# Hybrid gMLP and MoBA step: RMSNorm of the MoE router applied in the copies of rows, first expert pair's rows by one-hot products

## The reference

```python
def hier_moe(x, norm_g, w_rg, b_rg, w_re, b_re, w_gate, w_up, w_down):
    h = rms_norm(x, norm_g)
    lg = h @ w_rg + b_rg                       # 4 expert groups, top 1
    le = h @ w_re + b_re                       # 16 experts, top 2 inside the group
    ...
    for e in range(16):
        he = silu(h @ w_gate[e]) * (h @ w_up[e])          # 1024 -> 512
        y = y + gates[..., e:e + 1] * (he @ w_down[e])    # 512 -> 1024
```

## Time and profile before

| | |
|---|---|
| median of 3 runs | 1044.44 us (1040.47 to 1045.44) |
| profiled execution, own time | 1046.14 us |
| its span, first to last instruction | 1044.4 us |
| mean granted TensorE clock | 0.941 |
| TensorE matmul busy | 935.9 us, 90% |
| VectorE busy | 397.7 us, 38% |
| ScalarE busy | 158.9 us, 15% |
| GpSimd busy | 68.1 us, 7% |
| DMA | 327.42 MB, 313 GB/s mean |
| chain that ended last | PE 74%, VectorE 11%, DMA 6%, issue 5% |

### The profile page before, as it was taken

The page is one execution under the profiler, slowest core; times in us unless marked ns, Lnnn a source line. Parts: engine busy times, 40 slices in busy tenths (PEclk is TensorE's granted clock), DMA queues, the critical chain, the costliest instruction groups (busy, mean ns, idle before and its releaser), DMA issues.

```text
span 1044.4 us, 12577 instructions
## 1 busy us (share of the span) xinstructions
PE 935.9 (90%) x4275; PEld 530.1 (51%) x4275; DVE 397.7 (38%) x1828; ACT 158.9 (15%) x400; POOL 68.1 (7%) x93
## 2 busy tenths in 40 slices
PE   6999999977999988998999999766996999988897
PEld 5888888755444443344443334334765344444334
DVE  2235440051133322024697856887024133322014
ACT  2112010030100000002323220223221000000001
POOL 3000200021000000000000000000012000000000
PEclk9999999996999999999998999766996999999999
DMA  9903636063999999999669989998633899999991
GB/s 362 383 28 127 212 132 284 0 249 136 366 379 424 423 421 419 420 417 391 271 234 339 401 332 409 411 409 348 259 134 111 324 386 427 420 420 419 419 418 72
DMA packets 62431, 327.42 MB, mean 313 GB/s; under 512 B 6184, under 2 KB 6408, under 8 KB 51992
## 3 DMA queue, kind: packets, MB, share of 16 engines
q1 hardware_dynamic: 56752, 312.56, 74.5%
q0 software_dynamic: 4720, 11.77, 3.5%
q10 hardware_dynamic: 896, 2.30, 0.6%
HBM read 324.14 MB, written 6.52 MB: 317 GB/s over the span
## 4 chain that ended last, share of the span: by engine, by line
PE 74%; DVE 11%; DMA 6%; issue 5%; ACT 1%; SPq 1%; POOL 1%; ACTq 0%; DVEq 0%; POOLq 0%
PE bank L1197 20%; PE bank L979 11%; PE bank L1223 9%; PE bank L1279 6%; PE bank L1033 6%; DMA ring<-in_moe_w_gate 5%; DVE ring L1729 4%; PE bank L1178 4%; PE bank L1430 3%; PE bank L1394 2%; DVE xT L1672 2%; PE bank L1296 1%; PE bank L1104 1%; PE bank L974 1%; PE bank L1255 1%
## 5 line engine op out<-in xcount | busy, mean ns | idle before, releaser
L1197 PE MATMUL bank<-ring,arena 128*64 128x512 f32 x1024 | 234.7, 614 | 25.7 <-issue 24.3
L1197 PEld LDWEIGHTS bank<-ring,arena 128*64 128x64 f32 x1024 | 84.8, 141 | 172.8 <-issue 170.8
L979 PE MATMUL bank<-arena,ring 128*128 128x264 f32 x512 | 118.8, 389 | 0.1
L1223 PE MATMUL bank<-ring,arena 128*64 128x512 f32 x512 | 113.4, 595 | 2.0 <-ACT arena L740 2.0
L1729 DVE CUSTOM_DVE_ANT_0 ring<-ring,bank 128x128 f32<-128x128 f32 x512 | 110.8, 280 | 9.1 <-PE bank L1296 7.7
L1679 DVE TENSOR_TENSOR arena<-arena,bank 128x512 f32<-128x512 f32 x16 | 11.0, 688 | 248.7 <-PE bank L1197 248.7
L979 PEld LDWEIGHTS bank<-arena,ring 128*128 128x128 f32 x512 | 95.6, 190 | 15.9
L1279 PE MATMUL bank<-ring,arena 128*128 128x512 f32 x192 | 93.4, 637 | 1.2 <-ACT arena L848 1.2
L1223 PEld LDWEIGHTS bank<-ring,arena 128*64 128x64 f32 x512 | 36.2, 137 | 67.9 <-issue 65.5
L1178 PE MATMUL bank<-arena 128*128 128x264 f32 x256 | 63.4, 393 | 1.8 <-ACT arena L745 1.7
L1279 PEld LDWEIGHTS bank<-ring,arena 128*128 128x128 f32 x192 | 37.1, 202 | 52.1 <-issue 49.2
(11 more groups left out here) (245 smaller groups left out, 844.9 us busy)
## 6 DMA issues: line engine op xcount, KB each, us to landing
ring<-in_moe_w_gate SPq DMA_DIRECT2D x32, 2048.0 KB, 22.1
ring<-in_moe_w_up SPq DMA_DIRECT2D x32, 2048.0 KB, 17.8
ring<-in_moe_w_down SPq DMA_DIRECT2D x32, 2048.0 KB, 15.0
ring<-in_cache_k SPq DMA_DIRECT2D x64, 512.0 KB, 7.8
ring<-in_cache_v SPq DMA_DIRECT2D x64, 512.0 KB, 6.5
ring<-in_a_w_in SPq DMA_DIRECT2D x7, 2048.0 KB, 34.5
ring<-in_a_w_out SPq DMA_DIRECT2D x4, 2048.0 KB, 8.4
ring<-in_w_kv SPq DMA_DIRECT2D x4, 2048.0 KB, 16.0
```

Source lines behind the costliest of these rows:

```text
L979: return mm(bank[:, 0:T], slot(base + k // 2, 2)[:, k % 2, j * P:(j + 1) * P], hT[:, k, :], start=(k == 0), stop=(k == KT - 1))
L1197: last = mm(bank[64 * e:64 * e + 64, :], hg[:, int(odd), k, CAP * e:CAP * (e + 1)], slot(base + e, KT)[:, k, :], start=(k == 0), stop=(k = ...
L1223: last = mm(PB[4 + half][64 * e:64 * e + 64, :], heT[:, f, CAP * e:CAP * (e + 1)], slot(down[0] + e, FT)[:, f, 512 * half:512 * (half + 1) ...
```

## The change

- The reciprocal over 128x264 ahead of each router is gone, and the logits are copied unscaled. TensorE turns row 0 of the roots into a column per tile of tokens (three products with a 1), VectorE takes the reciprocals there (rs_t, one number for each token) and applies them in the step that adds the bias.
- GpSimd's eight scalings are gone. TensorE turns the unscaled stream, and ScalarE's copies into hr carry rs_t as the scale.
- The first pair's rows are not gathered from HBM. TensorE multiplies the one-hot of pair 0 with hr, three tiles of tokens for each half of the width, 512 columns at a time; ScalarE and VectorE copy the halves into gr, and the transposes of that pair follow from there. The second and later pairs are gathered as before. gr has moved to other columns of the arena.
- `keep_clock` is called with 4 in both places instead of 10 and 12, the first after the logits' transposes.
- The iota starts at 1, so that the rank needs no subtraction. The copies of gates for the first two pairs stand ahead of the rank, and the maximum behind the one-hots.

```diff
@@ constants
-    put("iota", np.tile(np.arange(CAP), (P, 1)))
+    put("iota", np.tile(np.arange(CAP) + 1.0, (P, 1)))
@@ GpSimd, moe
-                for k in range(KT):
-                    nc.gpsimd.tensor_tensor(hT[:, k, :], hT[:, k, :], rstd, ALU.mult).then_inc(h_made, 1)
...
                 pool.wait_ge(h_stored, 48 * (l + 1))
-                gather(0, 0)
-                gather(1, 1)
                 pool.wait_ge(many_set, l + 1)
...
-                    for i in range(2, NPAIR):
+                    for i in range(1, NPAIR):
                         gather(i, i % 2)
@@ ScalarE, moe
+                act.wait_ge(rstd_made, 2 * l + 1)
...
-                                         PB[4 + i % 4][0:n, :].rearrange("q (p k) -> q k p", k=KT), ACT.Copy)\
+                                         PB[4 + i % 4][0:n, :].rearrange("q (p k) -> q k p", k=KT), ACT.Copy,
+                                         scale=rs_t[0:n, t:t + 1])\
...
+                act.wait_ge(turned[l], 1)
+                nc.scalar.activation(gr[:, 0, 0:D // 2], PB[0][:, :], ACT.Copy).then_inc(hg_lo[l], 1)
@@ TensorE, moe
-                keep_clock(10)
                 pe.wait_ge(lgT_made, l + 1)
...
-                    last = tr(PB[2][0:n, t * 20:(t + 1) * 20], lgT[0:NGRP + NE, t0:t0 + n], ident[0:20, 0:20])
+                    tr(PB[3][0:n, t * 20:(t + 1) * 20], lgT[0:NGRP + NE, t0:t0 + n], ident[0:20, 0:20])
+                keep_clock(4, PB[0])
+                pe.wait_ge(rms_made, 2 * l + 1)
+                for t, (t0, n) in enumerate(TILES):
+                    last = mm(PB[3][0:n, 60 + t:61 + t], rms[0:1, t0:t0 + n], ones[0:1, 0:1], start=True, stop=True)
                 last.then_inc(lg_out, 1)
...
-                    pe.wait_ge(gr_load[l][b], 16 * (n + 1))
+                    if b == 0 and isinstance(n, int) and n == 0:
+                        pe.wait_ge(hg_lo[l], 1)
+                        pe.wait_ge(hg_hi[l], 1)
+                    else:
+                        pe.wait_ge(gr_load[l][b], 16 * (n + b))
...
                 pe.wait_ge(hr_kept, 6 * l + 6)
+                pe.wait_ge(hot_made[l], 1)
+                for half in range(2):
+                    for t, (_, n) in enumerate(TILES):
+                        last = mm(PB[half][:, :], hot[0:n, 0, t, :], hr[0:n, t, 512 * half:512 * (half + 1)],
+                                  start=(t == 0), stop=(t == 2))
+                    last.then_inc(turned[l], 1)
                 owners(0, 0)
                 owners(1, 1)
-                keep_clock(12)
+                keep_clock(4, PB[6])
@@ VectorE, moe
-                v.tensor_tensor(lgT[0:NGRP + NE, :], PB[3][0:NGRP + NE, 0:T], rstd[0:NGRP + NE, :], ALU.mult)\
-                    .then_inc(lgT_made, 1)
+                v.tensor_copy(lgT[0:NGRP + NE, :], PB[3][0:NGRP + NE, 0:T]).then_inc(lgT_made, 1)
...
+                ran(v.reciprocal(rs_t[:, 0:2], PB[3][:, 60:62]))
+                v.reciprocal(rs_t[0:NS, 2:3], PB[3][0:NS, 62:63]).then_inc(rstd_made, 1)
...
+                for t, (_, n) in enumerate(TILES):
+                    ran(v.scalar_tensor_tensor(out=lg[0:n, t, :], in0=PB[3][0:n, t * 20:(t + 1) * 20],
+                                               scalar=rs_t[0:n, t:t + 1], in1=bias[0:n], op0=ALU.mult, op1=ALU.add))
...
-                link(v.tensor_scalar(rank, rank, -1.0, None, ALU.add))
...
                 onehot(0, 0)
                 onehot(1, 1)
+                v.tensor_reduce(many[:, :], counted[:, 2, :], AX.X, ALU.max).then_inc(many_set, 1)
+                dve.wait_ge(turned[l], 2)
+                v.tensor_copy(gr[:, 0, D // 2:D], PB[1][:, :]).then_inc(hg_hi[l], 1)
                 owner_rows(0, 0, 0)
@@ VectorE, before and after each moe
-            normed(0, [])
...
-            normed(2, [])
```

More of the change, by code:

```diff
@@ L228, in small @@
             return region(ro - n, *shape)
-        gm, pg, mn, m1, m2, e2, w1, w2 = (small(3) for _ in range(8))
+        gm, pg, mn, m1, m2, e2, w1, w2, rs_t = (small(3) for _ in range(9))
         ohg, oh1, oh2, leg, le2, cand, ex = (small(3, 4) for _ in range(7))
@@ L1039, in _, with keep_clock @@
             sum_and_route(0, sqB, KT - 1)
-            def keep_clock(n):
+            def keep_clock(n, bank):
                 for _ in range(n):
-                    mm(PB[0][:, 0:P], ident, ident, start=True, stop=True)
+                    mm(bank[:, 0:P], ident, ident, start=True, stop=True)
             def turn_y(k):
@@ L1113, in moe @@
                 with pe.If(flag > LIMIT):
-                    pe.wait_ge(gr_load[l][0], 64)
+                    pe.wait_ge(gr_load[l][0], 48)
                     for k in range(KT):
                         if k >= 2:
-                            pe.wait_ge(hg_hi[l], k - 1)
+                            pe.wait_ge(hg_hi[l], k)
+                        elif k == 0:
+                            pe.wait_ge(hg_lo[l], 1)
+                            pe.wait_ge(hg_hi[l], 1)
                         for t, (t0, n) in enumerate(TILES):
@@ L1242, in moe @@
                 pe.nop()
-            moe(0, 0)
+            moe(0)
             def sample_part(m, h, h_base, banks):
@@ L1436, in _ @@
             sum_and_route(1, sqM, KT - 1)
-            moe(1, 3 * KT)
+            moe(1)
         @block.vector
@@ L1545, in moe @@
                 dve.wait_ge(lgT_out, l + 1)
-                v.tensor_tensor(lgT[0:NGRP + NE, :], PB[3][0:NGRP + NE, 0:T], rstd[0:NGRP + NE, :], ALU.mult)\
-                    .then_inc(lgT_made, 1)
-                link(v.tensor_copy(marks[:, :, :, 2], bc(const("token").unsqueeze(1), [P, 2, 3])))
+                v.tensor_copy(lgT[0:NGRP + NE, :], PB[3][0:NGRP + NE, 0:T]).then_inc(lgT_made, 1)
+                ran(v.tensor_copy(marks[:, :, :, 2], bc(const("token").unsqueeze(1), [P, 2, 3])))
+                ran(v.memset(rs_t, 0.0))
                 link(v.memset(lg, 0.0))
@@ L1551, in moe @@
                 bias = rbias[:, l, :]
-                ran(v.tensor_tensor(lg[:, 0:2, :], PB[2][:, 0:40].rearrange("p (t n) -> p t n", t=2),
-                                    bc(bias.unsqueeze(1), [P, 2, NGRP + NE]), ALU.add))
-                link(v.tensor_tensor(lg[0:NS, 2, :], PB[2][0:NS, 40:60], bias[0:NS], ALU.add))
+                ran(v.reciprocal(rs_t[:, 0:2], PB[3][:, 60:62]))
+                v.reciprocal(rs_t[0:NS, 2:3], PB[3][0:NS, 62:63]).then_inc(rstd_made, 1)
+                settle()
+                dve.wait_ge(rstd_made, 2 * l + 1)
+                for t, (_, n) in enumerate(TILES):
+                    ran(v.scalar_tensor_tensor(out=lg[0:n, t, :], in0=PB[3][0:n, t * 20:(t + 1) * 20],
+                                               scalar=rs_t[0:n, t:t + 1], in1=bias[0:n], op0=ALU.mult, op1=ALU.add))
+                settle()
                 lgg = lg[:, :, 0:NGRP]
@@ L1602, in moe @@
                                      bc(oh1.unsqueeze(2), g44), ALU.mult))
+                for b in range(2):
+                    v.tensor_copy(marks[:, b, :, 0:2], gates[:, :, 2 * b:2 * b + 2])
                 dve.wait_ge(rank_out, l + 1)
                 counted = PB[3][:, 0:3 * NE].rearrange("p (t e) -> p t e", t=3)
-                v.tensor_reduce(many[:, :], counted[:, 2, :], AX.X, ALU.max).then_inc(many_set, 1)
                 link(v.scalar_tensor_tensor(out=rank, in0=counted, scalar=1.0, in1=chose, op0=ALU.add, op1=ALU.mult))
-                link(v.tensor_scalar(rank, rank, -1.0, None, ALU.add))
                 def onehot(i, b):
@@ L1612, in onehot @@
                         dve.wait_ge(owner_out[l], i - 1)
-                    v.tensor_copy(marks[:, b, :, 0:2], gates[:, :, bass.ds(2 * i, 2)])
+                        v.tensor_copy(marks[:, b, :, 0:2], gates[:, :, bass.ds(2 * i, 2)])
                     v.tensor_tensor(hot[:, b, :, :].rearrange("p t (e s) -> p t e s", e=2),
@@ L1621, in owner_rows @@
                     dve.wait_ge(owner_out[l], i + 1)
-                    if not (isinstance(i, int) and i < 2):
-                        dve.wait_ge(gr_load[l][b], 16 * n)
+                    if not (isinstance(n, int) and n - 1 + b < 1):
+                        dve.wait_ge(gr_load[l][b], 16 * (n - 1 + b))
                     v.tensor_scalar(row_of[b][:, 0:1], PB[7][:, 2:3], 1.0 * EMPTY, None, ALU.add)
```

37 lines of the change are left out of this document (17 added, 20 removed).

## The result

| | before | after |
|---|---|---|
| median, side by side | 1045.06 us (7 runs, 1040.47 to 1051.35) | 1054.76 us (7 runs, 1049.37 to 1058.03) |
| profiled execution, own time | 1046.14 us | 1058.03 us |
| its span | 1044.4 us | 1056.2 us |
| mean granted clock | 0.941 | 0.932 |

A forecast was written before the change was run, and what follows sets the result against it. Product and load chains both start at each layer's first gate product, which the router bounds. Layer 0's -3.3 and layer 1's +0.9 gave -2.4 us, from the 1044.44 us median to 1042.0 us; range 1034 to 1047.

The forecast's parts named there:

- Lock of VectorE lifted, "-4.9": In each router, a VectorE step of 5.10 us no longer waits out GpSimd's eight scalings: 4.9 us less.
- ScalarE's "+0.3": Before the first one-hot, ScalarE's six row copies with a scale per partition add 0.3 us (bounds 0 and 0.5).
- Products, "7.6 us": Twelve one-hot passes per layer start at 1.2 GHz, reach full clock after 4.6 us: 7.6 us (all half clock 10.6).
- Dense products brought the clock back within 6 us both times: Argument against the low-clock rival: the clock rose 5.7 and 3.5 us after the gate products began.
- Owners, "1.1": After the one-hot products: pair 0's owner products at full clock 0.8 us, VectorE's two copies 0.3, together 1.1 us.
- Sending, flag and branch, "0.3 + 0.7 + 3.9": After the owners: sending 14 passes 0.3 us, flag load and register steps 0.7, branch over the all-tokens code 3.9.
- no bound of its own: Rival: the branch only waits for the queue to drain; -6.2 us, 1035.8 us, chance 0.12.
- From the branch to the gate product, "2.8": After the branch: transposes, their two copies and the first gate product at half clock, 2.8 us in each layer.
- The sum: Change in time to the first gate product: layer 0 -3.3 us, layer 1 +0.9 us, total -2.4 us.
- The claim that the router reaches the end one for one: Any shift of the first gate product in either layer shifts the kernel's end by the same amount.
- the clock stays low through the products and into the first pair: Rival: half clock in products, owners and first gate products costs 5.6 us per layer; 1053.2 us, chance 0.05.

The follow-up runs named there:

- fill_ahead: Changed kernel plus two groups of filler products (24 and 20 passes) where TensorE waits ahead of the one-hot products; 1041.89 us, ratio to before 1.0001.
- full_tile: Changed kernel with the third tile of tokens in the one-hot products read over all 128 partitions instead of 8; 1047.27 us, ratio to before 1.0042.
- full_early: all_three without the fillers ahead of ranks and products; 1036.05 us, ratio to before 0.9925.
- full_late: Changed kernel with the edits of full_tile and late_code together; 1041.36 us, ratio to before 0.9979.
- shift_code: Changed kernel with 24 nops at the start of TensorE's program; 1056.0 us, ratio to before 1.0132.
- late_code: Changed kernel with 12 filler products at the start of TensorE's program, to move its later code; 1046.22 us, ratio to before 1.0014.
- branch_early: Changed kernel with the second pair's owner products moved behind the branch, into both sides, and four fillers dropped; 1042.78 us, ratio to before 0.9999.
- all_three: Changed kernel with the edits of full_tile, fill_ahead and branch_early together; 1031.81 us, ratio to before 0.9882.
- norm_only: Kernel before with only the norm's part of the change, first pair still gathered, fillers of 10 and 12 kept; 1042.19 us, ratio to before 0.9976.
- norm_lean: norm_only without the ten fillers ahead of the transposes of logits; 1039.46 us, ratio to before 0.998.

## Why the prediction was wrong

- **Lock of VectorE lifted, "-4.9": right.** The step took 0.17 us, the first one-hot came 4.25 us earlier in layer 0 (forecast 4.4). Layer 1 gave 3.48: ScalarE's "+0.3" was 0.9 too small there, as its store's issue took 1.47 us instead of 0.53. The bound of 0.5 looked at the scale of the copies only, not at the stores between them.
- **Products, "7.6 us": the step that failed.** 11.47 and 11.46. "Dense products brought the clock back within 6 us both times" was read from gate products, and taken as a property of the clock. All twelve passes at half clock are 10.6 us by the forecast's own upper bound, 3.0 more than it counted. The other 0.9 the bound left out: passes of different shape follow each other less closely (5.97 against 5.39 us at full clock), and the earlier trace rows, with 9.0 us for 16 passes, gave 0.56 us each for 8 rows, not the 0.44 that was read as the same. Together 3.9 us more in each layer. That the clock sets the size is shown by fill_ahead. Without fillers, it rose midway in all six stretches of full_tile, full_early and full_late; with the 8-row tile, of eight (changed kernel, shift_code, late_code, branch_early) it stayed low in three, rose late in one and midway in four. The idle time just before the products does not explain this: where it was 2.9 us or less, the clock rose midway in five of five stretches without the 8-row tile and in one of five with it. That the 8-row tile is what makes it uncertain rests on these few counts and on three pairs of kernels that differ in it (1.0042 and 1.0088, 0.9925 and 0.9999, 0.9979 and 1.0014, the 8-row tile slower each time); it is likely, not shown. Whether by the gaps between its passes or by the few rows at work is open. The Trainium skill, TensorE: Matmul & The Clock Gate, Part 1, says that sustained matmul activity releases the throttle; three stretches here, of 11.5 us of products each, did not follow it.
- **Owners, "1.1": 1.8** in both layers, because they ran at the low clock (1.44 instead of 0.83).
- **Sending, flag and branch, "0.3 + 0.7 + 3.9": right.** From the second owners to the branch 0.9 and 0.8 us, the branch 3.83 and 3.76. branch_early shows that the branch is a delay of its own, which is what the rival "no bound of its own" denied.
- **From the branch to the gate product, "2.8": right in layer 0 (2.9), 6.9 in layer 1, the second step that failed.** The pause of 4.1 us was in no term and no rival. It goes when the code alone is moved (late_code). From that, and from its distance to the second transfer of code, which is that of the branch to the first, I read it as a second fetch, of the next piece of code, which the first transposes ran into; no run shows the fetch itself to be the cause. The Trainium skill, Runtime: NRT & Kernel Launch, Instruction fetch mechanics, describes refills in blocks of 16 KiB, purely sequential prefetch, and a stall at a taken branch that leaves the fetched window. The branch's 3.8 us and the transfer inside it (0.02 MB) agree; that execution can stall again behind the target is a reading of these traces.
- **The sum.** Layer 0: -3.3 + 3.9 + 0.7 = +1.3. Layer 1: +0.9 + 3.9 + 0.7 + 4.1 + 0.9 for the one-hot, less 0.5 in the hand-offs, the sending and the branch = +10.0. The claim that the router reaches the end one for one held on the whole: 11.3 of 11.8 us here, 14.0 against 13.4 in all_three; over all profiles the two differ by up to 3.6 us (shift_code: routers 6.8 us longer, span 10.4).
- **The rival "the clock stays low through the products and into the first pair"** gave 1053.2 us, close to the measured time, at a chance of 0.05. Its first half happened; of its second half nothing did (pair 0's 64 passes took 16.0 and 15.8 us, 16.9 and 15.7 before), and the pause filled the place. The chance was far too small: I had seen the clock rise twice under one kind of work, and took it for all but certain under another.
- Outside the routers the profiles vary without relation to an edit: from layer 0's first gate product to layer 1's last logit product 519.5 to 524.5 us, from layer 1's first gate product to the end 239.7 to 243.1. I have no cause for that, and it makes one profile's span a rough measure of an edit. The median of branch_early shows nothing of routers that were 9.8 us shorter in its profile (span 6.5 shorter). Its ten runs spread over 10 us; that their products ran now at one clock, now at the other, would explain it, but only one execution was profiled.

## What to carry to other kernels

Price work that is put on TensorE after a wait at half clock for its whole length too, not only at its start, unless something keeps it busy until then. Here fillers that stood in waits made 12 passes 5.5 us shorter than in the changed kernel, and some 2 us shorter than where the clock rose midway; with a ragged tile read over all partitions the clock rose in all six stretches. A branch over much code cost 3.3 to 6.3 us here from the moment that the sequencer reached it, so put it where products that are already queued cover it. And where a time moves by some us without a cause in the work, shift the code by a few real instructions before believing in one.

## What was not expected of the hardware

- The same twelve passes took 5.39, 5.97, 7.4 to 8.2, 10.5 or 11.5 us, by the clock and the shape of the third tile.
- The branch on TensorE took 3.3 to 4.6 us in layer 1 and 3.3 to 6.3 in layer 0, with seven over 5 us, all in layer 0 and reached between 234.6 and 243.6 us, while weights were loading; but norm_only, full_late, the kernel before and full_tile, which reached it between 241.2 and 243.1 us, took 3.3 to 3.9. What makes it longer was not tested.
- A pause behind a taken branch, which I read as a second code fetch, made the eight transposes 3.5 to 4.0 us longer (changed kernel, full_tile, shift_code); it was absent in the kernel before and in the ten others, and moving the code was enough to be rid of it.
- 24 nops left the pause where it was; 12 products at the same place did not.
- Stores of 1 MB, issued while weights moved at over 400 GB/s, landed 16 us after the last was issued, and so held a gather which took 3.3 us once it began (norm_lean). Issued 4 us later, in the kernel before, they landed no later.
